# Down-projections of a two-block network: first 128 tokens take 1024 columns, not 512, from fetched rows in six slots; VectorE weighs the acts, not GpSimd

## What is computed

```
def block(args):
    xt, it, gt = args                   # 128 tokens, their experts, their gates
    ue = jnp.take(u_tab, it, axis=0)
    ve = jnp.take(v_tab, it, axis=0)
    act = jax.nn.gelu(jnp.einsum('td,ted->te', xt, ue), approximate=False)
    return jnp.einsum('te,ted->td', (gt * act).astype(ve.dtype), ve)
```

## Time and profile before

| | us |
|---|---|
| median of 3 runs | 4018.9 (4017.02 to 4021.46) |
| span of the profiled execution, first to last instruction | 4015.3 |
| TensorE busy | 3961.1 (99%) |
| VectorE busy | 3285.0 (82%) |
| ScalarE busy | 2211.8 (55%) |
| GpSimd busy | 1104.6 (28%) |

### The profile page before, as it was taken

The page is one execution under the profiler, slowest core; times in us unless marked ns, Lnnn a source line. Parts: engine busy times, 40 slices in busy tenths (PEclk is TensorE's granted clock), DMA queues, the critical chain, the costliest instruction groups (busy, mean ns, idle before and its releaser), DMA issues.

```text
span 4015.3 us, 67806 instructions
## 1 busy us (share of the span) xinstructions
PE 3961.1 (99%) x21108; PEld 3330.9 (83%) x21108; DVE 3285.0 (82%) x5720; ACT 2211.8 (55%) x3915; POOL 1104.6 (28%) x1021
## 2 busy tenths in 40 slices
PE   8999999999999999999999999999999999999998
PEld 8978899888888877777789899988888887777776
DVE  6467677986999877999879987688699997777786
ACT  5445544555666655555564465455556665555555
POOL 4100010000122256666630002000012225666663
PEclk9999999999999999999999999999999999999999
DMA  6534665677666688898875544666766668888885
GB/s 224 178 113 142 200 177 192 211 219 214 202 200 198 199 299 288 284 330 309 307 242 183 180 157 153 200 199 213 219 200 199 199 201 280 292 288 304 287 288 189
DMA packets 319525, 899.44 MB, mean 224 GB/s; under 512 B 38256, under 2 KB 105584, under 8 KB 316016
## 3 DMA queue, kind: packets, MB, share of 16 engines
q1 hardware_dynamic: 285728, 812.75, 62.0%
q0 software_dynamic: 28672, 67.27, 5.2%
q10 hardware_dynamic: 4944, 17.06, 1.2%
HBM read 846.61 MB, written 50.33 MB: 223 GB/s over the span
## 4 chain that ended last, share of the span: by engine, by line
PE 89%; DVE 7%; ACT 1%; DMA 1%; issue 1%; DVEq 0%; ACTq 0%; SPq 0%
PE psum L464 12%; PE psum L466 11%; PE psum L465 11%; PE psum L523 9%; PE psum L525 9%; PE psum L524 9%; PE psum L1847 5%; PE psum L1848 5%; PE psum L1849 5%; DVE sb_w_lo L2452 3%; PE psum L2039 2%; PE psum L2041 2%; PE psum L2040 2%; PE psum L455 2%; PE psum L533 1%; DMA sb_raw<-in_v 1%
## 5 line engine op out<-in xcount | busy, mean ns | idle before, releaser
L2128 ACT CAST sb_w_hi<-sb_raw 128x512 fp32r<-128x512 f32 x2736 | 1692.9, 622 | 1531.8 <-PE psum L525 502.9
L2452 DVE TENSOR_TENSOR sb_w_lo<-sb_raw,sb_w_hi 128x512 fp32r<-128x512 f32 x2736 | 1918.5, 734 | 658.1 <-ACT sb_w_hi L2128 650.1
L464 PE MATMUL psum<-sb_w_hi,sb_act_hl 128*128 128x512 f32 x2048 | 800.0, 391 | 0.3
L466 PE MATMUL psum<-sb_w_lo,sb_act_hl 128*128 128x512 f32 x2048 | 799.1, 390 | 0.0
L465 PE MATMUL psum<-sb_w_hi,sb_act_hl 128*128 128x512 f32 x2048 | 798.3, 390 | 0.0
L523 PE MATMUL psum<-sb_w_hi,sb_act_hl 128*128 128x512 f32 x1792 | 708.1, 395 | 9.6 <-DVE sb_w_lo L2452 9.0
L525 PE MATMUL psum<-sb_w_hi,sb_act_hl 128*128 128x512 f32 x1792 | 698.5, 390 | 0.0
L524 PE MATMUL psum<-sb_w_lo,sb_act_hl 128*128 128x512 f32 x1792 | 698.2, 390 | 0.0
L2385 POOL TENSOR_TENSOR sb_work<-sb_scratch,sb_work 128x512 f32 x128 | 173.8, 1358 | 1389.0 <-ACT sb_scratch L597 1389.0
L1847 PE MATMUL psum<-sb_act_hl,sb_w_hi 128*128 128x256 f32 x1488 | 429.0, 288 | 26.9 <-DVE sb_w_lo L2452 13.8
L523 PEld LDWEIGHTS psum<-sb_w_hi,sb_act_hl 128*128 128x128 f32 x1792 | 336.3, 188 | 141.2 <-issue 73.8
(11 more groups left out here) (396 smaller groups left out, 4825.4 us busy)
## 6 DMA issues: line engine op xcount, KB each, us to landing
sb_raw<-in_u SPq DMA_DIRECT2D x512, 512.0 KB, 4.1
sb_raw<-in_v SPq DMA_DIRECT2D x512, 512.0 KB, 5.1
sb_raw<-in_w_z SPq DMA_DIRECT2D x82, 512.0 KB, 4.2
sb_raw<-in_w_gates SPq DMA_DIRECT2D x64, 512.0 KB, 3.7
acts_mid<-sb_up_acts SPq DMA_DIRECT2D x124, 256.0 KB, 5.1
sb_raw<-in_w_proj SPq DMA_DIRECT2D x56, 512.0 KB, 4.2
sb_raw<-in_w_q SPq DMA_DIRECT2D x48, 512.0 KB, 3.9
sb_raw<-in_w_branch SPq DMA_DIRECT2D x32, 512.0 KB, 4.0
```

Of the source, the lines that this page charges most:

```text
L464: pe.matmul(ps, h, w_hi[:, c, :], start=k == 0, stop=False)
L466: return pe.matmul(ps, h, w_lo[:, c, :], start=False, stop=k == 15)
L2128: act.copy(w_hi[:, c, :], raw[:, 2 * par + c // 2, (c % 2) * 512:(c % 2) * 512 + 512]).then_inc(hi_ready, 1)
L2452: dve.tensor_tensor(w_lo[:, c, :], raw[:, 2 * par + c // 2, (c % 2) * 512:(c % 2) * 512 + 512], w_hi[:, c, :].bitcast(F32), ALU.subtract). ...
```

## The change

Five things are changed together.

- `PICKED` is 1024: rows of 4 KB hold the last 1024 columns. Quarters 2 and 3 of the first token half get no dense products, so a tile has 18 matmuls where it had 21.
- A quad covers two banks (4 and 6), with eight matmuls where it had four.
- The 24 KB of row slots now hold six rows of 4 KB (`ROW_SLOTS`), one and a half quads. Row j of quad q goes to slot (4q + j) % 6 and waits for the quad whose row is there.
- `weigh` is VectorE's: `weigh(i + 1)` stands behind the subtraction of `lows(i)`.
- GpSimd only gathers, in the order of `PICKS` and no longer paced by tiles: two rows of the next quad, the four acts of this quad, the other two rows of the next.

The tiles after which the quads run are the same, and `place` is unchanged. At the end of a stage ScalarE waits for the last quad before it reads quarter 2, not quarter 3.

```diff
-PICKED = 512
-QUADS, QUAD_SLOTS = 32, 3
+PICKED = 1024
+QUADS, QUAD_SLOTS, ROW_SLOTS = 32, 3, 6
+PICKED_BANKS = [(0, 4, 0, 512), (512, 6, 0, 512)]
...
 PICKS = [("rows", 0, j) for j in range(4)]
 for quad_before in range(QUADS):
-    PICKS += [("rows", quad_before + 1, j) for j in range(4)] if quad_before + 1 < QUADS else []
+    PICKS += [("rows", quad_before + 1, j) for j in range(2)] if quad_before + 1 < QUADS else []
     PICKS += [("acts", quad_before, j) for j in range(4)]
-PICKS_AFTER = [[pick for k, pick in enumerate(PICKS) if pick_tile(k) == i] for i in range(128)]
+    PICKS += [("rows", quad_before + 1, j) for j in range(2, 4)] if quad_before + 1 < QUADS else []
...
-                    for t in range(QT) if c < 3 else (1,):
-                        ps = psum[:, 2 * c + t, :]
+                    for t in range(QT):
+                        n = min(512, D - PICKED - 512 * c) if t == 0 else 512
+                        if n <= 0:
+                            continue
+                        ps = psum[:, 2 * c + t, 0:n]
...
-                for j in range(4):
-                    mm = pe.matmul(psum[32 * j:32 * j + 32, 6, :], lone[:, n, j, :], picked[:, 4 * n + j, :],
-                                   start=q == 0, stop=False, skip_group_check=True)
+                for first, bank, at, n in PICKED_BANKS:
+                    for j in range(4):
+                        mm = pe.matmul(psum[32 * j:32 * j + 32, bank, at:at + n], lone[:, q % QUAD_SLOTS, j, :],
+                                       picked[:, (4 * q + j) % ROW_SLOTS, first:first + n],
+                                       start=q == 0 and at == 0, stop=False, skip_group_check=True)
...
             def lows(i, k, turn=True):
                 dve.wait_ge(c_hi, i + (128 * (blk - 1) + 1))
                 dve.tensor_tensor(act_hl[:, k % 2, T:2 * T], gate_e[:, i, :], act_hl[:, k % 2, 0:T].bitcast(F32), ALU.subtract).then_inc(c_lo, 1)
+                if i < 127:
+                    weigh(i + 1, (k + 1) % 2)
                 if turn:
                     turn_tile(i + 2, (k + 2) % 8)
                 low(i + b, (b + k) % 2)
+
+            def weigh(i, slot):
+                dve.wait_ge(acts_turned, i + (128 * (blk - 1) + 1))
+                e = gate_e[:, i, :].rearrange("p (t x g) -> p t g x", t=QT, g=4)
+                turned = turned_acts[:, slot, :].rearrange("p (t g x) -> p t g x", t=QT, g=4)
+                dve.tensor_tensor(e, turned, e, ALU.mult).then_inc(weighed, 1)
...
-                        if q >= QUAD_SLOTS and j == 0:
-                            pool.wait_ge(quad_used, QUADS * blk + q - QUAD_SLOTS + 1)
-                        pool.indirect_dma_start(picked[:, 4 * n + j, :], None, v_rows,
+                        used = (4 * q + j - ROW_SLOTS) // 4
+                        if used >= 0 and (j == 0 or (4 * q + j - ROW_SLOTS) % 4 == 0):
+                            pool.wait_ge(quad_used, QUADS * blk + used + 1)
+                        pool.indirect_dma_start(picked[:, (4 * q + j) % ROW_SLOTS, :], None, v_rows,
...
-                for i in range(128):
-                    weigh(i, i % 2)
-                    for kind, q, j in PICKS_AFTER[i]:
-                        pick(kind, q, j)
+                for kind, q, j in PICKS:
+                    pick(kind, q, j)
```

More of the change, by code:

```diff
@@ L58, in tile_bases @@
     return base, evac
-def pick_tile(k):
-    return 3 + k * 7 // 15
 def quad_tile(q):
-    return pick_tile(8 * q + 11) + 2
+    return 5 + (8 * q + 11) * 7 // 15
 PICKS = [("rows", 0, j) for j in range(4)]
 for quad_before in range(QUADS):
-    PICKS += [("rows", quad_before + 1, j) for j in range(4)] if quad_before + 1 < QUADS else []
+    PICKS += [("rows", quad_before + 1, j) for j in range(2)] if quad_before + 1 < QUADS else []
     PICKS += [("acts", quad_before, j) for j in range(4)]
-PICKS_AFTER = [[pick for k, pick in enumerate(PICKS) if pick_tile(k) == i] for i in range(128)]
+    PICKS += [("rows", quad_before + 1, j) for j in range(2, 4)] if quad_before + 1 < QUADS else []
 QUADS_AFTER = [[q for q in range(QUADS) if quad_tile(q) == i] for i in range(128)]
@@ L181, in build_two_blocks @@
         over_act = lambda name, row, shape: nc.alloc_sbuf_tensor_at("sb_" + name, shape, F32, offset=act_at + row * 2 * T * 4).ap()
-        picked = over_act("picked", 2, [P, 4 * QUAD_SLOTS, PICKED])
+        picked = over_act("picked", 2, [P, ROW_SLOTS, PICKED])
         lone = over_act("lone", 14, [P, QUAD_SLOTS, 4, 32])
@@ L519, in out_tile @@
                     pe.wait_ge(lo_ready, (i + b) * 4 + c + 1)
-                    for t in range(QT) if c < 3 else (1,):
-                        ps = psum[:, 2 * c + t, :]
+                    for t in range(QT):
[3 more added lines that the diff above has]
+                        ps = psum[:, 2 * c + t, 0:n]
                         c_h, c_l = (act_hl[:, par, lo + t * P:lo + t * P + P] for lo in (0, T))
-                        pe.matmul(ps, c_h, w_hi[:, c, :], start=first, stop=False, skip_group_check=True)
-                        pe.matmul(ps, c_h, w_lo[:, c, :], start=False, stop=False, skip_group_check=True)
-                        mm = pe.matmul(ps, c_l, w_hi[:, c, :], start=False, stop=False, skip_group_check=True)
+                        pe.matmul(ps, c_h, w_hi[:, c, 0:n], start=first, stop=False, skip_group_check=True)
+                        pe.matmul(ps, c_h, w_lo[:, c, 0:n], start=False, stop=False, skip_group_check=True)
+                        mm = pe.matmul(ps, c_l, w_hi[:, c, 0:n], start=False, stop=False, skip_group_check=True)
                     mm.then_inc(quarter_used, 1)
             def quad(q):
-                n = q % QUAD_SLOTS
                 pe.wait_ge(lone_ready, QUADS * (blk - 1) + q + 1)
-                for j in range(4):
-                    mm = pe.matmul(psum[32 * j:32 * j + 32, 6, :], lone[:, n, j, :], picked[:, 4 * n + j, :],
-                                   start=q == 0, stop=False, skip_group_check=True)
+                for first, bank, at, n in PICKED_BANKS:
[3 more added lines that the diff above has]
+                                       start=q == 0 and at == 0, stop=False, skip_group_check=True)
                 mm.then_inc(quad_used, 1)
@@ L665, in act_experts @@
                 act.wait_ge(quarter_used, 4 * (b + 127) + c + 1)
-                if c == 3:
+                if c == 2:
                     act.wait_ge(quad_used, QUADS * blk)
@@ L871, in dve_experts @@
             turn_tile(0, 0)
+            weigh(0, 0)
             turn_tile(1, 1)
@@ L2387, in _ @@
                 tiles(pool, 0, GROUPS, add_low)
[L2388 to L2394, removed]
                 v_rows = a[f"picked_v{blk + 1}"]
```

## The result

The changed kernel takes **4097.9 us** (median of 4 runs, 4097.24 to 4100.32) against 4019.2 of the kernel before in the same comparison: ratio 1.0199, interval 1.0187 to 1.0211. It is slower by 79 us, 97 above the forecast of 4001 and outside the range of 3945 to 4055. The profiled execution has a span of 4098.5 us.

A forecast was written before the change was run, and what follows sets the result against it. It took TensorE to bound the kernel, then the gather chain: stages of 640 and 656 us, 12 and 6 less, together 18 less, 3997 on the profiled span; 3.6 above that gives 4001 us, range 3945 to 4055.

The forecast's parts named there:

- transfers: Weight loads in both down-projection stages: wider rows delay weights by 6 us a stage; present stalls of 3 and 16 besides.
- The slack: Weight ring: slot round 10.0 us on average, less about 2.1 for splitting and issuing; landings may reach 6 or 8.
- the chain: GpSimd's gathers between quads: wake, eight gathers, landing, placing and quad take 17.9 to 18.4 us, holding up short intervals.
- The second rival: DMA engines become the bound in the down-projection stages, the weight ring running dry: 41 us more, 4060; chance 0.22.
- ceiling of 331 GB/s: Second rival's price: if the busiest 100 us' rate is what lasts, the stages take 660 and 695 us.
- the 342 and 351 GB/s of the forecast: Transfer rates the forecast needs in the second and first down-projection stages, 219 / 640 and 230 / 656.
- the scatter of the gathers: Between quads: varying gather times make long intervals 18.8 us on average and short ones 18.3.
- TensorE alone: Down-projection matmuls if nothing else bound: 594 us a stage, 110 less in all, with a quad at 2.23.
- wrong if other than 2.1 to 2.3: Sign for TensorE's quads: a quad taking any other time in us would show the forecast wrong in any case.
- The first rival: TensorE stays the bound in the down-projection stages: 3939, or 3909 without any chain; chance 0.2.
- The third rival: GpSimd's gathers get slower beside a busier VectorE: step 1.73 us, 74 us more, 4093; chance 0.08.
- The weighing: Moved to VectorE: 0.46 us a tile, low faster by 0.131, covered barely at 4.8 us a tile.

The follow-up runs named there:

- e1: The changed kernel with each gather fetching only 512 of a row's 1024 columns, used for both banks (part of the output wrong): 4015.8 us.
- e2: The changed kernel with a quad's four act gathers asked for ahead of the rows that wait for the quad before: 4013.0 us.
- e3: The changed kernel with both the half-width gathers of e1 and the early acts of e2: 3929.2 us.
- e9: The kernel e2 timed again over ten runs: 4021.8 us, ratio 1.0010 to the kernel before.
- e7: e6 with the rows of a quad spread over four tiles, each row waiting one tile more than the row before: 3985.9 us.
- e5: e2 with rows 0 and 1 of a quad held back, so that four rows don't go out together: 4012.9 us.
- e6: The changed kernel with 768 columns, eight row slots and acts gathered behind their own rows, all asked for once slots are free: 4005.0 us.
- e4: The kernel before with only the weighing moved from GpSimd to VectorE, gathers still paced by tiles: 4014.7 us, beside 4017.4.

## Why the prediction was wrong, point by point

- **The failed term is transfers.** The text put 6 us a stage, with 16 more in the first, on late weights, since "a landing may grow to some 6 or 8 us without harm". The landing grew to 6.6 and the harm was 78 and 52 us. The stalls' excess, 56 and 46, is 102; the miss on the spans is 101.5 (4098.5 against 3997). The other terms nearly cancel: 16 less for TensorE, 8 more for the chain, 3 more outside the two stages, and some 5 that the sums from starts leave out. Two things were wrong in that step. The slack was let go up to the mean over a stage, 10.0 less an estimate of 2.1; where no quad lies between two uses of a slot the text's own numbers gave 8.2 - 2.1 = 6.1, less than the median landing that came. And a median says nothing of late ones: ScalarE waited 83 and 77 times, up to 6.2 and 4.6 us at once. Of the 102, the wider rows' bytes are 64 (e1) to 82 (e2 against e3); the cause of the other 20 to 38 stays open. The sum for the second stage also leaves out the 3 us of present stalls that the text names beside it.
- **The rivals were set against each other where they add.** The second rival's mechanism was right in kind, weights short of their half of the engines and the ring run dry, but the text let either the chain or the transfers set the end, with 4060 for the second and 4001 for the first. e1, e2 and e3 show the sum: 82, 85 (76 by e9) and 169. My reading, argued and not measured by itself: while TensorE waits at a quad the ring can't run ahead by more than its four halves, so the wait doesn't pay for late weights of the tiles after it. Added by the text's own prices, the two give 660 + 40 and 695 + 40, 121 above the present 1314, so 4140: too much, by the size of the second.
- **Its price by a ceiling of 331 GB/s does not stand.** e2 moves more for as long as a hundred us:

```profile
1700.00:1800.00 100.00, 88.27 (x411) 62.42 (x409) 82.90 (x175) 55.00 (x100) 40.11 (x39) 1.00 0.98 371
```

  so 331 is not the most that the engines give. That the 342 and 351 GB/s of the forecast last for a whole stage no run shows; e2's 338 and 346 come nearest. What gave way was the landing time, and neither share nor rate of a stage tells it: weights landed after 6.6 us at 0.88 and 318 GB/s in the change, but after 5.1 at 0.89 and 307 in e3 and after 5.4 at 0.90 and 319 in e7. It goes with the rows: 6.6 to 6.9 with rows of 4 KB (the change, e2, e5), 5.7 and 5.8 with 3 KB in bursts (e6), 5.1 and 5.4 with 3 KB spread (e7), 5.1 to 5.3 with 2 KB (before, e1, e3). The Trainium skill ("DMA: Bandwidth & Descriptors", "Specifications") gives about 358 GB/s to a core, half of a stack's 716. These 371 lie above it, e2's 338 and 346 over whole stages below, so the traces don't show it as a ceiling. (219 MB at 358 are 612 us; the text's 610 is a slip of 2.)
- **The chain was right in kind, and its sum partly by luck.** Wake 0.31 (0.30 said), steps 1.32 in the chain shown (1.42), last act 6.46 (5.4), placing 0.49 (0.48), quad 1.92 (2.07): 18.5, for 17.9 to 18.4. The cheaper steps and the dearer landing offset each other. The eight short intervals of the second stage that end in a wait are 17.9 to 20.3, 18.7 on average (18.3 said). The long ones are 18.8 to 23.3 (18.8 said), but by the stalls inside their tiles: one alone ends in a wait, of 0.4, so the scatter of the gathers that the text gave them cost next to nothing; e2 and e9 price the whole at 85 and 76, for 80 said. Of this the lower clock is 23, which the text didn't have, and the waits are 65, less than said.
- **TensorE alone was nearly right**, 586 a stage for 594: a quad costs 1.94, not 2.23, and "wrong if other than 2.1 to 2.3" goes against the text. By the same sum of starts a quad of the kernel before cost 1.09, where the text had 1.23, and the second bank adds 0.85, where it had 1.00.
- **The first rival** (TensorE the bound, 3939 or 3909) fell by both costs, and e3, with neither the chain nor the wider rows, comes to 3929.
- **The third rival's 4093 fits the time by accident.** Its mechanism, slower gathers, is refuted by GpSimd's groups in the second stage, as in the earlier trace rows:

```profile
L2417 POOL DMA_INDIRECT sb_picked_acts<-acts_mid,sb_slots x128 | 136.2, 1064 | 49.0 <-issue 47.2 <-DVE sb_slots L856 1.8
L2410 POOL DMA_INDIRECT sb_picked<-in_picked_v,sb_slots x128 | 132.3, 1034 | 376.5 <-PE psum L532 319.5 <-issue 29.3 <-PE psum L524 27.7
```

  They got shorter, 1.06 and 1.03 for 1.14 and 1.10, with a VectorE that weighs. So what the Trainium skill ("SBUF — State Buffer", "SBUF: two separate sides") says of descriptors that GpSimd can't write until VectorE releases the shared port made no difference that these runs show.
- **The weighing** took 0.62 for 0.46, and `low` came to 0.69 as said:

```profile
L2453 DVE TENSOR_TENSOR sb_w_lo<-sb_raw,sb_w_hi 128x512 fp32r<-128x512 f32 x511 | 336.9, 688 | 125.2 <-ACT sb_w_hi L2137 124.3
L834 DVE TENSOR_TENSOR sb_work<-sb_scratch,sb_work 128x256 f32<-128x256 f32 x126 | 78.5, 623 | 0.0
```

  The term was too small by 0.16 a tile, outside the "0.4 to 0.5" of the text; at the pace of the kernel before it costs nothing (e4).

What stays open: a deeper ring of weights at 1024 columns was not tried, so it is not settled how late landings and a ring of two tiles share in e2's 75 and 56 us. e5 excludes only that it takes a burst of four rows to make them; why the landing rises with the size of the rows and falls with spreading at 3 KB is not shown.

## What to carry to other kernels

Two costs that stopped the same engine at different places added here; take only the larger of them if you can show that the wait for one gives the other time to catch up. When bytes go onto DMA engines that are 0.85 busy, don't price them by bandwidth or by the engines' mean share alone: at a share of 0.88 to 0.90 weights landed after 5.1, 5.4 or 6.6 us, by the size and spread of the other transfers. Take the slack of a ring in its shortest round and against late landings, not in the mean. Where fewer buffers make a gather wait, ask first for what doesn't need the buffer: e2 took off some 80 us by the order of requests alone.

## What the runs showed of the hardware

- Behind a wait of 4.07 us TensorE's granted clock was 0.50 for at least 5.6 us, and the quad in it took 3.64 instead of 1.92 us: with the slower matmuls behind it, this wait of 4 cost nearly 7. In e3, without such waits, the clock was 1.00 in both stages.
- VectorE's product of 128x256 whose gates are read and written with a step of four elements took 0.62 us, where the subtraction of the same shape on plain operands took 0.42 (e4: 617 and 422 ns). That the step makes the difference is not shown by itself.
- Eight column-group matmuls cost TensorE 1.94 us, four cost 1.09 by the same sum (0.32 ahead, 1.00 to the next matmul, less one step): the second bank adds 0.85.
- Over a whole stage, 512 KB of weights landed after 5.4 us (median) beside spread rows of 3 KB at 319 GB/s (e7), and after 6.6 beside rows of 4 KB at 318 GB/s (the change).
